# The residue value columns by seven block products, in turns with the plain ones

## The chip, the cores and the metric

The kernel runs on one core of a Trainium2 chip. The metric is device microseconds of one execution; the kernel before took 1865.35 us, the median of three runs (1864.94 to 1866.59).

## What is computed

A decoder trunk of two layers on x of 512 positions by 1024 channels, in float32. In each layer h = RMSNorm(x) is projected by one matrix w_in to queries and keys of a dilated attention (three head groups with dilations 1, 4 and 16), their values, and queries, keys and values of a retention, besides gates:

```
hn = rmsnorm(x, g_mix)
proj = hn @ w_in
qa, ka, va, qr, kr, vr, gr, ga, gb = jnp.split(proj, SPLIT_POINTS, axis=-1)
```

The attention's values va are three groups of 512 columns. Group 0 (dilation 1) is used in the order of the positions. Groups 1 and 2 (dilations 4 and 16) are used by residue: their tiles hold the positions t with the same t mod 4. The retention's values vr are 1024 columns in plain order. After that come the attention, the retention, w_a, w_b, w_o and a squared-ReLU MLP (w_up, w_down), which the change does not touch.

## The kernel before

**Products.** Every float32 operand is split in a high part, rounded to the matmul's fp32r format, and a low part, the rest. A product is three matmuls (high by high, high by low, low by high) that add up in PSUM. A weight unit is 128 partitions by 2048 columns (1 MB). ScalarE copies its two halves to w_hi (2 x 1.05 us) and VectorE subtracts to w_lo; there are two pairs of such buffers, so a unit is converted while the one before it is multiplied (`value_high`, line 844, waits for the end of unit n-2; `value_low`, line 1355). Raw weights land in the one buffer w_raw, each half of which may be loaded again when its low half is done.

**The value stage** is the first of each layer: a list of units, V_SEQ (line 76). G is group 0's value columns, two units of 48 matmuls of 128x512. P is vr, 1024 rows by 1024 columns: it is done by seven block products in Strassen's manner. Each of the seven takes a quarter of the activations, or a difference of quarters, by a quarter of the weights, or a sum of quarters, in 24 matmuls (4 k tiles x 2 position tiles x 3). R is groups 1 and 2 of va, in plain form: four halves (`residues_half`, line 2130) of 48 matmuls, whose stationary operand steps over h by 4 elements. The order is G G P1 R0 P5 R1 P6 P3 R2 P7 R3 P2 P4.

**The sums.** Quarters of h are subtracted on VectorE (`value_sum`, line 1361), then split by ScalarE (`set_high`, 859) and VectorE (`set_low`, 1376) into one of three sets. Products share PSUM banks: each result is read in between (`value_read` on ScalarE, 866, after products 1, 5, 6 and 4; `value_finish` on VectorE, 1382, after 3, 7 and 2), and `value_ready` (2095) makes TensorE wait for that read before it adds on or opens the bank anew. The sums of weight quarters are made by accumulating DMAs from GpSimd's queue (`add_values`, 1191) in two slots, gh[0] for products 1, 5, 6, 4 and gh[1] for 3 and 7; each waits until the slot's last content has been split. That is 4 accumulates of 1 MB a layer.

**SP's queue** issues in order: the units G, the two slots, x to scratch (two parts), raw R0 and R1, the store of rstd (after `rms_spread`) and its read back by residue, raw R2, R3, the scratch stores of vr (`vR_away`), raw P2, the tables, and then the first query and key pairs. VectorE's and ScalarE's loops over the stage (lines 1409 and 876) give, for each unit under way, the conversion of the next one and then reads, finishes and sums, all in order. TensorE takes the units one after the other (line 2155).

Of the kernel before, what the change touches and what calls it, by code (L numbers as in the profile page):

```python
# [35 lines left out]
P = 128  # L36
F32 = mybir.dt.float32
# [15 lines left out]
def trunk(nc, a):  # L53
# [54 lines left out]
    def by_raw(j):  # L108
        if j < P0:
            return V_SEQ[j - V0][0] != "P" or V_SEQ[j - V0][1] == 2  # L110
        return j < M0 or M_SEQ[j - M0][0] == "U" or plain(*M_SEQ[j - M0][1:])
# [22 lines left out]
    def last_read(l, i):  # L134
        return l * VO + TB + {3: 2, 7: 4, 2: 6}[i]

    def v_adds(l, i):
        return (l * 3 + {5: 1, 6: 2, 4: 3}[i] if i != 7 else l + 1) * 16

# [16 lines left out]
    with ExitStack() as ctx:  # L156
# [19 lines left out]
        nrstd = sb("nrstd", [P, TB], F32)  # L176
# [98 lines left out]
        diag = at("N", "diag", [P, TB, P], F32)  # L275
        hn = at("N", "hn", [P, 2, S], F32)
        relu = at("N", "relu", [P, 2, S], F32)
        gh = [at("N", f"gh{i}", [P, 2048], F32) for i in range(2)]
# [33 lines left out]
        def vbank(l, i):  # L312
            return ((sc, yr) if l > 0 else (yr, sc))[i in (5, 3, 2)]

        rbank = [pt[:, 0:S], pt[:, S:2 * S], pj[1][:], pj[0][:]]
# [85 lines left out]
        v_in = [sem(f"v_in{i}") for i in range(2)]  # L401
        v_added = [sem(f"v_added{i}") for i in range(2)]
        v_res = sem("v_res")
        v_first = sem("v_first")
# [93 lines left out]
        def _(sp):  # L498
# [35 lines left out]
            for l in range(0, DEPTH):  # L534
# [23 lines left out]
                def value_raw(kind, i):  # L558
                    d = raw[:].rearrange("p (k c) -> p k c", k=4)
                    v = value_block("R", i % 2, i // 2) if kind == "R" else value_block("P", 1, 0)  # L560
                    load(v_unit(l, kind, i), [(d[:, m:m + 2, :], v[:, m:m + 2, :]) for m in (0, 2)])

                def value_slot(slot):
                    sp.dma_start(gh[slot][:].rearrange("p (k c) -> p k c", k=4),
                                 value_block("P", slot, slot)).then_inc(v_in[slot], 16)
# [21 lines left out]
                def vR_away(part, m, b0):  # L587
                    if part < 3:
                        sp.wait_ge(v_out, last_read(l, (3, 7, 2)[part]))
                    else:  # L590
                        sp.wait_ge(v_first, first_read(l, 4))
# [28 lines left out]
                vR_away(1, 1, 2)  # L620
                sp.wait_ge(rot_out, l * 8 * PAIRS + 1)
# [127 lines left out]
        def _(act):  # L749
# [93 lines left out]
            for l in range(0, DEPTH):  # L843
                def value_high(s):
                    n = l * LU + V0 + s
                    act.wait_ge(mm_done, n * 2 - 2 + MM_CREDIT)
                    kind, i = V_SEQ[s] if s < VN else ("Q", 0)
                    if kind != "P" or i == 2:
                        hi_halves(n, n % 2)
                        return  # L850
                    slot = int(i in (3, 7))
                    if i in (1, 3):
                        act.wait_ge(v_in[slot], l * 16 + 16)
                    else:
                        act.wait_ge(v_added[slot], v_adds(l, i))
                    for c in HALVES:
                        nc.scalar.copy(w_hi[n % 2][:, c], gh[slot][:, c]).then_inc(hi_done, 1)  # L857

                def set_high(i):
                    p = V_SUMS.index(i)  # L860
                    if p >= SETS:
                        act.wait_ge(mm_done, v_unit(l, "P", V_SUMS[p - SETS]) * 2 + 2 + MM_CREDIT)
                    act.wait_ge(v_sum, l * 4 + p + 1)
                    nc.scalar.copy(a_sets[(p + 1) % SETS][0][:], ssum_v[p % 2]).then_inc(v_set_hi, 1)

                def value_read(i):
                    act.wait_ge(mm_done, v_unit(l, "P", i) * 2 + 2 + MM_CREDIT)
                    act.wait_ge(nrstd_done, l + 1)
# [3 lines left out]
                    for b in range(2):  # L872
                        nc.scalar.activation(vP[:, b0 + b, m], vbank(l, i)[:, b * S:(b + 1) * S], ACT.Copy,
                                             scale=by[:, b0 + b:b0 + b + 1]).then_inc(v_first, 1)

                for s in range(1, VN):
                    kind, i = V_SEQ[s]
                    if s == 2:
                        rms(l)
                    if V_SEQ[s - 1] in (("P", 1), ("P", 5), ("P", 6)):  # L880
                        value_read(V_SEQ[s - 1][1])
                    value_high(s + 1)
                    if (kind, i) in (("P", 1), ("R", 0), ("P", 5), ("P", 6)):
                        set_high({("P", 1): 5, ("R", 0): 6, ("P", 5): 3, ("P", 6): 7}[kind, i])
                value_read(4)
# [299 lines left out]
        def _(pool):  # L1185
# [4 lines left out]
            for l in range(0, DEPTH):  # L1190
                def add_values(i):
                    slot = int(i == 7)
# [3 lines left out]
                    nc.gpsimd.dma_start(gh[slot][:].rearrange("p (k c) -> p k c", k=4),  # L1196
                                        w_in_v[l, :, 4 * h:4 * h + 4, V_AT["P"] + m, :],
                                        accum_op=ALU.add).then_inc(v_added[slot], 16)

                for i in (5, 6, 4, 7):  # L1200
                    add_values(i)
# [41 lines left out]
        def _(dve):  # L1243
# [107 lines left out]
            for l in range(0, DEPTH):  # L1351
# [3 lines left out]
                def value_low(s):  # L1355
                    n = l * LU + V0 + s
                    kind, i = V_SEQ[s] if s < VN else ("Q", 0)
                    for hf in range(2):
                        lo_half(n, n % 2, hf, gh[int(i in (3, 7))] if kind == "P" and i != 2 else raw)

                def value_sum(i):
                    p = V_SUMS.index(i)
                    if p == 0:
                        dve.wait_ge(hn_done, 2 * l * KT + KT)
                        dve.wait_ge(sum_done, (2 * l + 1) * (KT - 1))
                    else:
                        dve.wait_ge(v_sum, l * 4 + p)
                    if p >= 2:
                        dve.wait_ge(v_set, l * 4 + p - 1)
                    a11, a12, a21, a22 = (h32[:, 4 * kh:4 * kh + 4, 2 * P * th:2 * P * th + 2 * P]  # L1370
                                          for th in range(2) for kh in range(2))
                    x0, x1, op = {5: (a21, a22, ALU.subtract), 6: (ssum_v[0], a11, ALU.subtract),
                                  3: (ssum_v[1], a12, ALU.add), 7: (a11, a21, ALU.subtract)}[i]
                    nc.vector.tensor_tensor(ssum_v[p % 2], x0, x1, op).then_inc(v_sum, 1)

                def set_low(i):
                    p = V_SUMS.index(i)
                    to_hi, to_lo = a_sets[(p + 1) % SETS]
                    dve.wait_ge(v_set_hi, l * 4 + p + 1)
                    nc.vector.tensor_tensor(to_lo[:], ssum_v[p % 2], to_hi[:], ALU.subtract).then_inc(v_set, 1)  # L1380

                def value_finish(i):
                    m, b0 = {2: (0, 0), 3: (1, 0), 7: (1, 2)}[i]
                    by, op = nrstd if i == 7 else rstd, ALU.add if i == 2 else ALU.subtract
                    dve.wait_ge(mm_done, v_unit(l, "P", i) * 2 + 2 + MM_CREDIT)
                    dve.wait_ge(v_first, first_read(l, {2: 1, 3: 6, 7: 5}[i]))
                    for b in range(2):
                        to = vP[:, b0 + b, m]
# [1089 lines left out]
```

## Time and profile before

| | |
|---|---|
| median of three runs | 1865.35 us |
| the profiled execution, in all | 1867.26 us |
| its span, first to last instruction | 1865.3 us |
| mean granted TensorE clock | 0.998 |
| TensorE, weight loads, VectorE, ScalarE, GpSimd busy | 1855.0, 1559.6, 1290.2, 832.5, 140.6 us |
| DMA moved | 236.9 MB, mean 127 GB/s |

A row of a timeline is the start in us, the duration, engine and line, operation, tile written from tiles read, and the count that was merged; the idle time before it and what ended it stand in brackets. DMA-issuing instructions stand on the queue that issues them (SPq, POOLq). A row of DMA issues has tile and source, queue, count, size of each, and the us from issue to landing. A windows row has the stretch, its length, the busy us and number of instructions of TensorE, its weight loads, VectorE, ScalarE and GpSimd, then the granted clock (1.00 is 2.4 GHz), the mean busy share of the 16 DMA engines and GB/s. A share slightly over 1 comes of packets that lie over the window's edge or each other.

### The profile page before, as it was taken

How to read it: one execution, taken by the hardware profiler on the slowest of the kernel's cores; microseconds unless marked ns; L12 is line 12 of the kernel's file. 1: busy time of each engine (PE TensorE's matmuls, PEld its weight loads, DVE VectorE, ACT ScalarE, POOL GpSimd, SP SyncE). 2: the span in 40 equal slices, each digit the busy share in tenths (PEclk: the TensorE clock that was granted, in tenths of full speed). 3: DMA queues.
4: the chain of work that ended last, by engine and by line, in shares of the span. 5: the costliest groups of instructions: out<-in, count | busy, mean ns of one | idle time of the engine just before them, and what ended most of it. 6: DMA issues, size and time to landing. Idle time of an engine off the chain costs nothing.

```text
span 1865.3 us, 22969 instructions
## 1 busy us (share of the span) xinstructions
PE 1855.0 (99%) x9016; PEld 1559.6 (84%) x9016; DVE 1290.2 (69%) x1882; ACT 832.5 (45%) x1234; POOL 140.6 (8%) x112
## 2 busy tenths in 40 slices
PE   9999999999999999999999999999999999999998
PEld 8988888888888888888889888888888888888886
DVE  6466878877446576776984668788675575667778
ACT  6335465465223343443543365554642234434345
POOL 0001111100000000000000112112000000000000
PEclk9999999999999999999999999999999999999999
DMA  8553233233433465557765433233243334655675
GB/s 255 125 167 110 75 86 105 84 94 96 133 96 125 117 148 133 145 135 189 174 181 149 137 92 97 77 111 96 69 147 100 104 113 113 136 142 140 142 205 137
DMA packets 213295, 236.92 MB, mean 127 GB/s; under 512 B 12354, under 2 KB 162626, under 8 KB 211908
## 3 DMA queue, kind: packets, MB, share of 16 engines
q1 hardware_dynamic: 191348, 192.64, 32.6%
q0 software_dynamic: 21120, 41.95, 13.3%
q8 instruction: 71, 1.16, 0.3%
q10 hardware_dynamic: 720, 0.87, 0.2%
q14 instruction: 36, 0.29, 0.1%
HBM read 222.72 MB, written 10.62 MB: 125 GB/s over the span
## 4 chain that ended last, share of the span: by engine, by line
PE 98%; DVE 1%; ACT 1%; DMA 0%; issue 0%; SPq 0%
PE pj L1986 21%; PE pj L1988 21%; PE pj L1987 21%; PE yr L2342 2%; PE yr L2346 2%; PE yr L2344 2%; PE sc L2342 2%; PE sc L2346 2%; PE sc L2344 2%; PE pt L2342 2%; PE pt L2344 2%; PE pt L2346 2%; PE sc L2190 1%; PE pt L2147 1%; PE pj L2147 1%; PE pt L2149 1%
## 5 line engine op out<-in xcount | busy, mean ns | idle before, releaser
L1986 PE MATMUL pj<-h_hi,w_hi 128*128 128x512 f32 x1408 | 554.0, 393 | 0.0
L1988 PE MATMUL pj<-h_hi,w_lo 128*128 128x512 f32 x1408 | 548.4, 389 | 0.0
L1987 PE MATMUL pj<-h_lo,w_hi 128*128 128x512 f32 x1408 | 548.2, 389 | 0.0
L759 ACT CAST w_hi<-w_raw 128x1024 fp32r<-128x1024 f32 x268 | 270.7, 1050 | 243.3 <-PE pj L1988 56.9
L1257 DVE TENSOR_TENSOR w_lo<-w_raw,w_hi 128x1024 fp32r<-128x1024 f32 x271 | 321.0, 1220 | 80.4 <-ACT w_hi L759 79.0
L1986 PEld LDWEIGHTS pj<-h_hi,w_hi 128*128 128x128 f32 x1408 | 264.3, 188 | 57.1 <-issue 1.9
L1988 PEld LDWEIGHTS pj<-h_hi,w_lo 128*128 128x128 f32 x1408 | 264.3, 188 | 56.0
L1987 PEld LDWEIGHTS pj<-h_lo,w_hi 128*128 128x128 f32 x1408 | 264.5, 188 | 53.9 <-issue 0.5
L1257 DVE TENSOR_TENSOR w_lo<-gh,w_hi 128x1024 fp32r<-128x1024 f32 x104 | 122.5, 1219 | 12.4 <-ACT w_hi L857 9.9
L1210 POOL TENSOR_TENSOR rcos<-rot,tables 128x512 f32<-128x512 f32 x64 | 88.5, 1384 | 524.1 <-ACT rot L893 465.6
L1067 ACT ACTIVATE relu<-pj 128x512 f32<-128x512 f32 x64 | 38.2, 597 | 182.6 <-PE pj L1988 182.6
L774 ACT CAST w_hi<-gh 128x1024 fp32r<-128x1024 f32 x80 | 80.0, 1050 | 87.5 <-PE yr L2346 35.5
L1752 DVE TENSOR_TENSOR u<-relu,rstd_all 128x512 f32<-128x512 f32 x64 | 44.1, 689 | 99.0 <-ACT relu L1067 98.9
L1218 POOL DMA_DIRECT2D gh<-in_w_down x26 | 33.4, 1283 | 937.3 <-DVE w_lo L1257 907.7
L893 ACT COPY rot<-pj 128x512 f32<-128x512 f32 x48 | 27.9, 582 | 102.1 <-PE pj L1988 56.3
L1451 DVE TENSOR_TENSOR swp<-swp,tables 128x512 f32<-128x512 f32 x64 | 65.0, 1015 | 4.4 <-ACT swp L897 2.7
L2342 PE MATMUL sc<-w_hi,a_hi 128*128 128x512 f32 x160 | 62.4, 390 | 0.3 <-DVE tables L1819 0.3
L2344 PE MATMUL sc<-w_lo,a_hi 128*128 128x512 f32 x160 | 62.3, 389 | 0.0
L2346 PE MATMUL sc<-w_hi,a_lo 128*128 128x512 f32 x160 | 62.2, 389 | 0.0
L2342 PE MATMUL yr<-w_hi,a_hi 128*128 128x512 f32 x160 | 62.2, 389 | 0.0
L2344 PE MATMUL yr<-w_lo,a_hi 128*128 128x512 f32 x160 | 62.2, 389 | 0.0
L2346 PE MATMUL yr<-w_hi,a_lo 128*128 128x512 f32 x160 | 62.2, 389 | 0.0
(352 smaller groups left out, 3199.5 us busy)
## 6 DMA issues: line engine op xcount, KB each, us to landing
w_raw<-in_w_in SPq DMA_DIRECT2D x139, 512.0 KB, 4.7
w_raw<-in_w_up SPq DMA_DIRECT2D x64, 512.0 KB, 4.6
gh<-in_w_down POOLq DMA_DIRECT2D x26, 1024.0 KB, 8.9
gh<-in_w_down SPq DMA_DIRECT2D x16, 1024.0 KB, 5.1
w_raw<-in_w_down SPq DMA_DIRECT2D x20, 512.0 KB, 5.2
gh<-in_w_in POOLq DMA_DIRECT2D x8, 1024.0 KB, 8.6
w_raw<-in_w_b SPq DMA_DIRECT2D x16, 512.0 KB, 4.4
w_raw<-in_w_o SPq DMA_DIRECT2D x16, 512.0 KB, 3.6
```

The lines of the kernel that those rows point to most:

```text
L759: nc.scalar.copy(w_hi[s][:, c], raw[:, c]).then_inc(hi_done, 1)
L774: nc.scalar.copy(w_hi[n % 2][:, h], gh[slot][:, h]).then_inc(hi_done, 1)
L1210: nc.gpsimd.tensor_tensor(rcos[:], rot[:], cosA if u < 3 else cosR, ALU.mult).then_inc(rot_cos, 1)
L1257: nc.vector.tensor_tensor(w_lo[s][:, c], src[:, c], w_hi[s][:, c], ALU.subtract).then_inc(lo_done, 1)
L1451: nc.vector.tensor_tensor(swp[:], swp[:], sinA if u < GROUPS else sinR, ALU.mult).then_inc(rot_sin, 1)
L1752: nc.vector.tensor_tensor(to, relu[:, o, :], rstd_all[:], ALU.mult).then_inc(relu_scaled, 1)
L1986: nc.tensor.matmul(out, w_hi[s][:, wc], acts[0], start=first, stop=False)
L1987: nc.tensor.matmul(out, w_hi[s][:, wc], acts[1], start=False, stop=False)
L1988: return nc.tensor.matmul(out, w_lo[s][:, wc], acts[0], start=False, stop=last)
L2342: nc.tensor.matmul(out, hi[:, k, t], w_hi[s][:, w], start=opens and k == 0, stop=False, skip_group_check=not opens)
L2344: nc.tensor.matmul(out, hi[:, k, t], w_lo[s][:, w], start=False, stop=False, skip_group_check=not opens)
L2346: return nc.tensor.matmul(out, lo[:, k, t], w_hi[s][:, w], start=False, stop=k == 3, skip_group_check=not opens)
```

## The change

R is gone. The residue columns of va are a second seven-product matrix, Q, that takes turns with P in the order 1 2 5 6 3 7 4: G G P1 Q1 P2 Q2 P5 Q5 P6 Q6 P3 Q3 P7 Q7 P4 Q4. Q1, Q2 and Q4 read h by residue as R did; the other four read sums which VectorE makes from h by residue, in four instructions each, and which lie contiguous. Q's banks are pj and pt. There are four weight slots: P's and Q's for 1, 5, 6, 4 and for 7; the new ones lie in the MLP's tiles and in the tables' tile, whose load now waits for Q7. Products 2 and 3 come raw. GpSimd issues eight accumulates. P2's finish and Q2's now stand before P5 and Q5, and rstd by residue is needed, negated too, from Q1's read on.

```
-    V_SEQ = [("G", 0), ("G", 1), ("P", 1), ("R", 0), ("P", 5), ("R", 1), ("P", 6), ("P", 3), ("R", 2), ("P", 7),
-             ("R", 3), ("P", 2), ("P", 4)]
+    V_SEQ = [("G", 0), ("G", 1)] + [(kind, i) for i in (1, 2, 5, 6, 3, 7, 4) for kind in "PQ"]
+    V_SUMS = [(kind, i) for i in (5, 6, 3, 7) for kind in "PQ"]
+    def v_slot(kind, i):
+        return 2 * (kind == "Q") + (i == 7)
+        v_slots = [gh[0][:], gh[1][:], v_q[:], tables[:].rearrange("p i s -> p (i s)")]
+        def vbank(l, kind, i, b):
+            if kind == "P":
+                return ((sc, yr) if l > 0 else (yr, sc))[i in (5, 3, 2)][:, b * S:(b + 1) * S]
+            return pj[b][:] if i in (5, 3, 2) else pt[:, b * S:(b + 1) * S]
...
 SP's queue:
-                value_slot(0)
-                value_slot(1)
+                value_slot("P", 1)
+                if l > 0:
+                    sp.wait_ge(a_ready, l * LD)
+                value_slot("Q", 1)
                 x_out(0)
-                value_raw("R", 0)
+                value_raw("P", 2)
                 x_out(1)
-                value_raw("R", 1)
+                value_slot("P", 7)
+                if l > 0:
+                    sp.wait_ge(d_turned, l * KT)
+                value_slot("Q", 7)
                 rstd_away()
                 rstd_by_residue()
-                value_raw("R", 2)
-                value_raw("R", 3)
+                value_raw("Q", 2)
+                value_raw("P", 3)
+                value_raw("Q", 3)
                 vR_away(0, 1, 0)
-                value_raw("P", 2)
                 vR_away(1, 1, 2)
+                sp.wait_ge(lo_done, v_unit(l, "Q", 7) * 2 + 2 + UNIT_CREDIT)
                 sp.wait_ge(rot_out, l * 8 * PAIRS + 1)
                 sp.dma_start(tables[:], a["tables"]).then_inc(tables_in, 16)
...
 ScalarE, during unit s:
+                    value_high(s + 1)
+                    if V_SEQ[s - 1][1] in (1, 5, 6) and V_SEQ[s - 1][0] == "P":
+                        value_read(*V_SEQ[s - 1])
+                    if s == V_SEQ.index(("Q", 2)):
+                        value_read("Q", 1)
+                    elif V_SEQ[s - 1] in (("Q", 5), ("Q", 6)):
+                        value_read(*V_SEQ[s - 1])
+                    if s + 2 < VN and V_SEQ[s + 2] in V_SUMS:
+                        set_high(*V_SEQ[s + 2])
...
 GpSimd:
-                    pool.wait_ge(lo_done, v_unit(l, "P", {5: 1, 6: 5, 4: 6, 7: 3}[i]) * 2 + 2 + UNIT_CREDIT)
+                    if i != 7:
+                        pool.wait_ge(lo_done, v_unit(l, kind, {5: 1, 6: 5, 4: 6}[i]) * 2 + 2 + UNIT_CREDIT)
                     pool.wait_ge(v_in[slot], l * 16 + 16)
-                for i in (5, 6, 4, 7):
-                    add_values(i)
+                for i in (5, 7, 6, 4):
+                    for kind in "PQ":
+                        add_values(kind, i)
...
 VectorE, during unit s:
+                    value_low(s + 1)
+                    if s == V_SEQ.index(("Q", 2)):
+                        dve.wait_ge(rstd_res, l * 16 + 16)
+                        negated(TB)
+                    if V_SEQ[s - 1][1] in (2, 3, 7) and V_SEQ[s - 1][0] != "G":
+                        value_finish(*V_SEQ[s - 1])
+                    if s + 2 < VN and V_SEQ[s + 2] in V_SUMS:
+                        set_low(*V_SEQ[s + 2])
+                    if s + 3 < VN and V_SEQ[s + 3] in V_SUMS:
+                        value_sum(*V_SEQ[s + 3])
...
 TensorE, value_ready:
+                    elif i in (5, 4):
+                        pe.wait_ge(v_last[kind], last_read(l, {5: 2, 4: 7}[i]))
                     else:
-                        pe.wait_ge(v_first, first_read(l, {6: 1, 7: 6, 3: 5}[i]))
+                        pe.wait_ge(v_first[kind], first_read(l, {6: 1, 7: 6, 3: 5}[i]))
```

## Rows read from the trace of the kernel before

**Rows 1.** Page: busy time, share of the span and instructions of each engine.
```profile
PE 1855.0 (99%) x9016; PEld 1559.6 (84%) x9016; DVE 1290.2 (69%) x1882; ACT 832.5 (45%) x1234; POOL 140.6 (8%) x112
```

**Rows 2.** Waits of TensorE, the longest: waited-for, us in total, times, longest.
```profile
PE pj L1950 <- DMA x_nat<-in_x: 1.2, 1, 1.2
```

**Rows 3.** Windows of the two value stages, layer 0 and layer 1.
```profile
35.30:119.70 84.40, 84.40 (x369) 77.68 (x370) 50.69 (x59) 29.84 (x34) 5.30 (x4) 1.00 0.58 142
957.30:1041.80 84.50, 84.50 (x371) 77.77 (x371) 49.39 (x57) 29.61 (x33) 3.85 (x3) 1.00 0.57 140
```

**Rows 4.** Timeline of TensorE: the first matmuls of R0, P5, R1, P6, P3.
```profile
41.65 0.62 PE L2147 MATMUL pt<-w_hi,h_hi 128*128 128x512 f32 x1
53.15 0.40 PE L2122 MATMUL sc<-w_hi,a_hi 128*128 128x512 f32 x1
58.63 0.40 PE L2147 MATMUL pt<-w_hi,h_hi 128*128 128x512 f32 x1
69.91 0.40 PE L2122 MATMUL yr<-w_hi,a_hi 128*128 128x512 f32 x1
75.36 0.39 PE L2122 MATMUL sc<-w_hi,a_hi 128*128 128x512 f32 x1
```

**Rows 5.** Timeline of VectorE and ScalarE: split, finish, plain and strided add; cast, read.
```profile
61.06 2.36 DVE L1257 TENSOR_TENSOR w_lo<-gh,w_hi 128x1024 fp32r<-128x1024 f32 x2 [2.01 <-ACT w_hi L857]
81.00 1.41 DVE L1389 SCALAR_TENSOR_TENSOR x<-sc,rstd,x 128x512 f32<-128x512 f32 x2 [0.85 <-PE sc L2126]
127.97 0.69 DVE L1456 TENSOR_TENSOR qk<-rcos,swp 128x512 f32<-128x512 f32 x1
138.77 1.06 DVE L1458 TENSOR_TENSOR qk<-rcos,swp 128x512 f32<-128x512 f32 x1
70.11 2.00 ACT L857 CAST w_hi<-gh 128x1024 fp32r<-128x1024 f32 x2 [8.12 <-PE pj L2149]
75.56 1.27 ACT L873 ACTIVATE x<-yr,rstd 128x512 f32<-128x512 f32 x2 [2.50 <-PE yr L2126]
```

**Rows 6.** Timeline of SP's queue: store of rstd and read back, both layers.
```profile
43.36 0.31 SPq L569 DMA_DIRECT2D rstd_scratch<-rstd_all  x1
46.92 0.37 SPq L573 DMA_DIRECT2D rstd<-rstd_scratch  x1
964.71 0.25 SPq L569 DMA_DIRECT2D rstd_scratch<-rstd_all  x1
967.60 0.36 SPq L573 DMA_DIRECT2D rstd<-rstd_scratch  x1
```

**Rows 7.** DMA issues at 35.95, 94.62, 41.62, 79.05, 80.18, 1814.39, 1817.22, in that order.
```profile
gh<-in_w_in POOLq DMA_DIRECT2D x1, 1024.0 KB, 8.6
w_raw<-in_w_in SPq DMA_DIRECT2D x1, 512.0 KB, 3.5
w_raw<-in_w_in SPq DMA_DIRECT2D x1, 512.0 KB, 4.3
w_raw<-in_w_in SPq DMA_DIRECT2D x1, 512.0 KB, 6.3
w_raw<-in_w_in SPq DMA_DIRECT2D x1, 512.0 KB, 6.5
u<-in_w_down POOLq DMA_DIRECT2D x1, 1024.0 KB, 12.5
w_raw<-in_w_down SPq DMA_DIRECT2D x1, 512.0 KB, 9.5
```

**Rows 8.** Windows: accumulate alone, beside plain loads, loads alone, beside again.
```profile
67.20:71.40 4.20, 4.20 (x20) 3.91 (x19) 1.29 (x2) 1.29 (x2) 0.00 (x0) 1.00 1.11 204
80.80:83.20 2.40, 2.40 (x12) 2.40 (x12) 1.41 (x2) 0.00 (x0) 0.00 (x0) 1.00 1.11 211
84.50:86.50 2.00, 2.00 (x10) 2.00 (x10) 1.00 (x1) 1.92 (x2) 0.00 (x0) 1.00 1.03 371
1819.00:1826.00 7.00, 7.00 (x32) 5.79 (x32) 6.70 (x7) 2.96 (x3) 0.00 (x0) 1.00 1.06 235
```

More of the change, by code:

```diff
@@ L400, in trunk @@
         st_lo = sem("st_lo")
[L401 to L404, printed above, removed]
+        v_in = [sem(f"v_in{i}") for i in range(4)]
+        v_added = [sem(f"v_added{i}") for i in range(4)]
+        v_first = {kind: sem(f"v_first_{kind}") for kind in "PQ"}
+        v_last = {kind: sem(f"v_last_{kind}") for kind in "PQ"}
         v_sum = sem("v_sum")
@@ L588, in vR_away @@
                     if part < 3:
-                        sp.wait_ge(v_out, last_read(l, (3, 7, 2)[part]))
+                        sp.wait_ge(v_last["P"], last_read(l, (3, 7, 2)[part]))
                     else:
-                        sp.wait_ge(v_first, first_read(l, 4))
+                        sp.wait_ge(v_first["P"], first_read(l, 4))
                     to = vr_scratch[:, 2 * m:2 * m + 2].rearrange("p h (b c) -> p b h c", b=TB)
@@ L1356, in value_low, with value_sum @@
                     n = l * LU + V0 + s
-                    kind, i = V_SEQ[s] if s < VN else ("Q", 0)
+                    kind, i = V_SEQ[s] if s < VN else ("G", 0)
                     for hf in range(2):
-                        lo_half(n, n % 2, hf, gh[int(i in (3, 7))] if kind == "P" and i != 2 else raw)
-                def value_sum(i):
-                    p = V_SUMS.index(i)
+                        lo_half(n, n % 2, hf, raw if kind == "G" or i in (2, 3) else v_slots[v_slot(kind, i)])
+                def value_sum(kind, i):
+                    p = V_SUMS.index((kind, i))
                     if p == 0:
@@ L1374, in value_sum @@
-                    nc.vector.tensor_tensor(ssum_v[p % 2], x0, x1, op).then_inc(v_sum, 1)
-                def set_low(i):
-                    p = V_SUMS.index(i)
+                    if p >= 2:
+                        dve.wait_ge(v_set, l * 8 + p - 1)
+                    if kind == "P":
+                        a11, a12, a21, a22 = (h32[:, 4 * kh:4 * kh + 4, 2 * P * th:2 * P * th + 2 * P]
+                                              for th in range(2) for kh in range(2))
+                        to = ssum_v[0]
+                    else:
+                        a11, a12, a21, a22 = (h32[:, 4 * kh:4 * kh + 4, :].rearrange("p k (m r) -> p k r m", r=4)
+                                              [:, :, 2 * th:2 * th + 2] for th in range(2) for kh in range(2))
+                        to = ssum_v[1].rearrange("p k (r m) -> p k r m", r=2)
@@ new lines, in value_sum @@
+                    x0, x1, op = {5: (a21, a22, ALU.subtract), 6: (to, a11, ALU.subtract),
+                                  3: (to, a12, ALU.add), 7: (a11, a21, ALU.subtract)}[i]
+                    if kind == "P":
+                        nc.vector.tensor_tensor(to, x0, x1, op).then_inc(v_sum, 1)
+                        return
+                    for k in range(4):
+                        mm = nc.vector.tensor_tensor(to[:, k], x0[:, k], x1[:, k], op)
+                    mm.then_inc(v_sum, 1)
@@ L1400, in first_values, with negated @@
                                                 ALU.mult).then_inc(v_out, 1)
[L1402 to L1407 removed]
+                def negated(c0):
+                    nc.vector.tensor_scalar(nrstd[:, c0:c0 + TB], rstd[:, c0:c0 + TB], -1.0, None,
+                                            ALU.mult).then_inc(nrstd_done, 1)
                 for s in range(1, VN):
[L1410 removed]
                     if s == 2:
@@ L2155, in _ @@
                 for kind, i in V_SEQ[V_U:]:
[L2156 removed]
+                    if (kind, i) == ("Q", 1):
                         spread(l)
[L2158 to L2162 removed]
+                    value_product(kind, i)
+                pe.wait_ge(v_last["Q"], (l + 1) * VO)
                 def queries_keys(i, behind=None):
@@ L2178, in scores @@
                         pe.wait_ge(rot_out, J * 8 + 6 + 1)
-                        pe.wait_ge(v_out, (l + 1) * VO)
-                        pe.wait_ge(v_first, (l + 1) * VF)
+                        for kind in "PQ":
+                            pe.wait_ge(v_first[kind], (l + 1) * VF)
+                            pe.wait_ge(v_last[kind], (l + 1) * VO)
                         pe.wait_ge(u_out, J * 4 + 4)
```

190 lines of the change are left out of this document (70 added, 120 removed).

## The prediction

> **What bounds the kernel now.** I read the page's totals first. TensorE is busy 1855.0 us, 99% of the span [rows 1], and its longest wait is 1.2 us, in the start-up [rows 2]. The path is TensorE's queue, so every matmul removed is worth its issue interval, until one of its feeders is late. The question is which feeder that will be. The value stage, which the change rebuilds, lasts 84.4 us in each layer. VectorE is busy 50.7 us of it, ScalarE 29.8 us, the DMA share is 0.58, and TensorE is gapless at the full granted clock, 1.00 [rows 3]. The timeline of TensorE gives the units: R0 starts at 41.65, P5 at 53.15, R1 at 58.63, P6 at 69.91, P3 at 75.36 [rows 4]; the stage ends at 119.7. A P product (24 matmuls) is 5.45 us (69.91 to 75.36), 0.227 us a matmul. A residue half (48 matmuls, 4-element steps in the stationary operand) is 11.28 us (58.63 to 69.91), 0.235 us a matmul; the first one took 11.50. The weight conversion for the next unit may start only when the unit before the present one has ended, as there are two pairs of buffers. In the long R halves that leaves 11.3 us for about 3.6 us of work; that slack is what the change spends.
>
> **Term A, the matmuls.** Removed in each layer: 4 R halves, 11.50 + 3 x 11.28 = 45.3 us. Added: 7 Q products. Three (1, 2, 4) read h by residue, at half a residue half: 5.85 + 2 x 5.64 = 17.1 us. Four read the contiguous sums: 4 x 5.45 = 21.8 us. Sum 38.9 us, so -6.4 us a layer. With nothing late the starts in layer 0 become: Q1 41.65, P2 47.50, Q2 52.95, P5 58.59, Q5 64.04, end 113.3.
>
> **What it costs beside TensorE.** Per layer three more units are converted, with 2.0 us on ScalarE and 2.3 on VectorE each [rows 5] (the row of two splits has 2.36, but the next instruction starts some 0.07 before such an end; the finish's 1.41 counts as 1.34 and a single split or sum as 1.14 likewise). There are four more sums, of four instructions each on residue-strided inputs. No row has one. The same 1024 elements contiguous take half of the 2.36 us of two splits, 1.2, while 512 elements with both inputs strided take 1.06 against 0.69 contiguous (the same rows). So a Q sum lies between 1.2 (no penalty) and 2.4 us (four times 0.53 and as many starts). I take 2.1, twice the strided row. Four more activation splits cost 1.05 us on ScalarE (half a cast's row) and 1.14 on VectorE each; two more finishes of 1.34, less eight R evictions. VectorE comes to 14 splits 32, 8 set lows 9, sums 4.6 + 8.4, six finishes 8, and the first values, norm and tables about 8: 70 us in a stage of 78. It fits as a total, but not as an order. Plain DMA: the weights for Q are two slots and two raw loads (4 MB, as R's four raw loads). New are four more accumulating DMAs of 1 MB, 8 in place of 4.
>
> **Term B, Q2's weights.** On SP's queue the raw load for Q2 now stands behind the store of rstd and its read back. Before, R1's load stood ahead of them (issued 41.62 and 42.76, ahead of 43.36). The store was issued at 43.36 and the read at 46.92 [rows 6], so SP stands 3.56 us. In the changed kernel rstd_all comes at about 42.6 (the spread is the same matmul, and VectorE is free of one sum), the read back at 46.2, and the two halves of Q2's load at 46.6 and 47.0. How long they take depends on what is under way. With no accumulate beside it such a half landed in 3.5 us, and at the tail of one in 4.3 [rows 7]. With one accumulate beside them for about 4 of the us they took 6.3 and 6.5. With one all the time (issued 1817.22) both took 9.5 [rows 7]. The reason is in the windows: an accumulate alone keeps the DMA share at 1.11 with 204 GB/s, and with plain loads beside it the sum is 211 to 235 GB/s, while plain loads alone move 371 [rows 8]. In the changed kernel accumulates for P5, Q5, P7, Q7 are queued from 35.95 on, the last three with no wait between them (at 42.1, when Q1 is split, then 43.4 and 44.7). 4.2 MB at 204 GB/s are 20.6 us; with the last part of slot Q7, Q2 and P3's load (2.3 MB) beside them at 235 GB/s, 27.7 us. So DMA is saturated from 38 to about 66, around Q2's load. I take the 9.5 row: the second half lands at T = 56.5.
>
> What hangs on T is VectorE's order, for P5 can't start before P2 is finished (its banks), and that finish now stands last in a chain: the cast of Q2's second half 1.05, ScalarE's high half of P5's sum 1.05 behind it, VectorE's low half 1.14, the sum for Q5 2.1, the split for P5 2.3, the negation 0.1, the finish 1.34, and about 0.4 for four handovers: 9.5 us. P5 starts at 56.5 + 9.5 = 66.0 in place of 58.6: **+7.4**. (Q2's own late start lies inside this.) At 3.5 to 4.3 us for the half it would be T = 51 and +2, or nothing if the sum is cheap; at T = 59, +10.
>
> **Term C, Q5.** It may not start before Q2 is finished. From P5's start: read of Q1 1.2 [rows 5] and set high 1.05 on ScalarE, then on VectorE set low 1.14, the sum for P6 1.14, the split for Q5 2.3, the finish 1.34, with handovers about 6.95 us, and P5 lasts 5.45: **+1.5**. It holds even where DMA is instant, as VectorE has no slack here; bounds 0.9 and 2.
>
> **Term D, P3 to P7.** P3 and Q3 are consecutive raw units. From P3's first split to Q3's: load 4.6, cast 1.05, split 1.22, handovers 0.2 = 7.0 us against 5.45, unless P3's was early, which VectorE (now behind) and Q6's accumulate forbid: +1.4. ScalarE, in order, then delays P7 by about the same, 1.3. The sum is **+2.7**; 0 if the accumulates run unhindered, 5 if they lag. P6 and Q6: the accumulate for P6 is issued at about 65, when P5 is split, and needs 8.6 [rows 7] plus 2.4 for cast and split: 76, against a start at 77.5. Hidden, by 1.5 us.
>
> Moved at no cost: the tables' load now waits for Q7's split and P7's finish, but is needed only for the first rotary some 6 us into the next stage; its splits are done before. The scratch stores of vP come later in units but no later against the end, and half of them are waited for only by the retention. The first R wait for four first values stays, as Q1's. PE's group waits on v_last are C and B.
>
> **Sum.** Layer 0: -6.4 + 7.4 + 1.5 + 2.7 = +5.2. Layer 1: the same stage and the same order. The store and read stood 2.9 us (964.71 to 967.60) in place of 3.56 [rows 6], so +4.6. Together +9.8 us. The profiled execution took 1867.3 us, 2 us outside its span and 1.9 above the median of 1865.35, so 1877 on its scale; on the median's, **1875 us**.
>
> Two rules of the Trainium skill bear on B. The trace shows 8.6 us for an accumulate of 1 MB. The page "DMA: Bandwidth & Descriptors", section "Anatomy of one DMA", gives 2.0 us plus the bytes over 436 GB/s for a DMA of this path, an estimate of 4.4 us here. By that nothing would queue and B and D would vanish; it is the first rival. The measurement disagrees for accumulates. The trace also shows plain loads slowed from 3.5 to 6.3 and 9.5 us beside one. The same page, "Issuing engines are not separate DMA queues", says that all issuers share the same 16 engines and interleave; the trace agrees.
>
> **Rivals.** (1) DMA keeps pace, faster: Q2's halves land in 4.3 us as R1's did at 41.62, so T = 51.3, P5 is late by 2.2, C 1.5, D 0: -2.7 a layer, **1860**; with no stall but C, -4.9, 1855.5. For it: the total DMA share is only 0.58, and R1's load met one accumulate's tail. Against it: three accumulates back to back, not one. It decides at T = 54.0 with D gone, at 51.3 with D whole. Chance 0.22. (2) Q2's load fares as the one at 79.05, 6.5 us: T = 53.5, B 4.4, D between 0 and 2.7: -0.5 to +2.2 a layer, **1867**. Chance 0.13. (3) The accumulates become the bound. Each behaves as the one at 1814.39, which took 12.5 us beside plain loads [rows 7]; four in a row from 38 then end at about 78, P6's lands at 84.5 and P6 starts at 86.9 in place of 77.5: +9.4 for D's 2.7: +11.9 a layer, **1889**. For it: 8 accumulates where 4 were. Against it: after 66 few plain loads are left. Chance 0.18. The forecast itself (1868.5 to 1884) has 0.47. That Q is not done by seven products at all is excluded by the diff.
>
> **Numbers.** A measurement of this kernel tells 0.2%, 3.7 us, from no change. Faster beyond it: rival 1, 0.22. Within: rival 2, 0.13. Slower: 0.65. The range 1857 to 1890 leaves out the best end of rival 1 and the upper half of 3.
>
> **What would show it.** A: 24 fewer 128x512 matmuls a layer in the value lines, at the same interval. B: a TensorE gap before the sixth unit (Q2) and before P5, with ScalarE waiting for w_raw from DMA, landings of 8 to 10 us at SP's load after the rstd read, and the P5 gap ended by VectorE's L1389 operation. C: a gap of 1 to 2 us before Q5, ended by the same line. D: gaps before Q3 and P7. A DMA share near 1 for 28 us. I am wrong if Q2's second half lands within 4.5 us of its issue, if the Q sums take 1.2 us, or if accumulates queued together move more than 204 GB/s.

## The result, and the profile after

The changed kernel took **1888.9 us** (median of 4 runs, 1888.0 to 1891.1) against 1865.8 for the kernel before on the same chip: ratio 1.0127, 95% interval 1.0115 to 1.0139, or +23.1 us. The forecast was 1875, +9.8. The direction was right, and the stalls stand where they were put, but the net loss is 2.4 times the forecast: the forecast had 11.6 us of stalls in layer 0 against 6.4 us of saved matmuls, and 18.0 came. The profiled execution took 1888.3 us. One execution of run 6 below took 3111 us at a mean granted clock of 0.556, a slower state of the chip, and its median leaves that one out.

The totals of the page of the changed kernel answer to [rows 1]:

```profile
PE 1851.6 (98%) x8968; PEld 1542.4 (82%) x8968; DVE 1329.4 (70%) x1932; ACT 861.6 (46%) x1270; POOL 151.3 (8%) x120
```

There are 48 matmuls fewer, 24 a layer, but TensorE's share of the span fell. Its waits, where there had been 1.2 us at most [rows 2] (waited for, us in total, times, longest):

```profile
PE pj L2151 <- DVE w_lo L1279: 16.0, 4, 6.2
PE sc L2151 <- DVE x L1422: 3.5, 1, 3.5
PE yr L2151 <- DVE x L1422: 2.8, 1, 2.8
```

The first is Q2's and Q3's weights, in both layers. The other two are P5, waiting for the finish of P2 (L1422; L1389 before). The windows of the two value stages (length, busy time and instructions of PE, PEld, DVE, ACT, POOL, granted clock, DMA share, GB/s) answer to [rows 3]:

```profile
33.04:129.08 96.04, 83.40 (x346) 69.98 (x346) 66.75 (x80) 42.99 (x50) 10.45 (x8) 0.93 0.76 175
966.71:1062.66 95.95, 83.33 (x346) 69.45 (x346) 66.71 (x80) 43.34 (x51) 9.05 (x7) 0.95 0.74 167
```

So 11.6 and 11.5 us more than 84.4 and 84.5: together the 23.1 of the medians. Nothing outside the value stages moved. (In the one profiled execution of before the stage starts 2.3 us later than here, and over 2 us later than in any other trace. That execution took 1.9 us more than its median, so the delay is taken to be its own.) TensorE's timeline in layer 0, the first matmuls of Q1, P2, Q2, P5, Q5, P6, Q3 and P7, answers to [rows 4]:

```profile
39.43 0.60 PE L2151 MATMUL pt<-w_hi,h_hi 128*128 128x512 f32 x1
45.27 0.40 PE L2151 MATMUL sc<-w_hi,h_hi 128*128 128x512 f32 x1
57.11 0.79 PE L2151 MATMUL pj<-w_hi,h_hi 128*128 128x512 f32 x1 [6.20 <-DVE w_lo L1279]
67.90 0.77 PE L2151 MATMUL sc<-w_hi,a_hi 128*128 128x512 f32 x1 [3.51 <-DVE x L1422]
76.26 0.39 PE L2151 MATMUL pj<-w_hi,a_hi 128*128 128x512 f32 x1
81.70 0.39 PE L2151 MATMUL yr<-w_hi,a_hi 128*128 128x512 f32 x1
99.64 0.47 PE L2151 MATMUL pj<-w_hi,a_hi 128*128 128x512 f32 x1 [1.46 <-DVE w_lo L1279]
106.20 0.47 PE L2151 MATMUL yr<-w_hi,a_hi 128*128 128x512 f32 x1 [0.84 <-DVE w_lo L1279]
```

The gap before Q2 is 6.2 us, the one before P5 is 3.5, and then P5 lasts 8.36 us without a gap, where such a product takes 5.45. SP's and POOL's queues, against [rows 6]. The start is the moment of issue. The last row merges six loads, the halves for Q2, P3 and Q3, issued between 44.86 and 92.5:

```profile
33.74 1.44 POOL L1217 DMA_DIRECT2D gh<-in_w_in  x1 [32.58 <-DVE w_lo L1279]
40.06 1.29 POOL L1217 DMA_DIRECT2D v_q<-in_w_in  x1 [4.89 <-DVE w_lo L1279]
40.82 1.84 POOL L1217 DMA_DIRECT2D gh<-in_w_in  x1
44.02 1.28 POOL L1217 DMA_DIRECT2D tables<-in_w_in  x1 [1.35 <-DMA tables<-in_w_in]
40.43 0.31 SPq L575 DMA_DIRECT2D rstd_scratch<-rstd_all  x1
44.45 0.37 SPq L579 DMA_DIRECT2D rstd<-rstd_scratch  x1
44.86 47.62 SPq L520 DMA_DIRECT2D w_raw<-in_w_in  x6
```

And how long they took to land (issued 33.74, 40.06, 40.82, 44.02; last Q2's two halves, a median), against [rows 7]:

```profile
gh<-in_w_in POOLq DMA_DIRECT2D x1, 1024.0 KB, 12.6
v_q<-in_w_in POOLq DMA_DIRECT2D x1, 1024.0 KB, 12.2
gh<-in_w_in POOLq DMA_DIRECT2D x1, 1024.0 KB, 18.6
tables<-in_w_in POOLq DMA_DIRECT2D x1, 1024.0 KB, 22.4
w_raw<-in_w_in SPq DMA_DIRECT2D x2, 512.0 KB, 11.4
```

The accumulates landed at 46.3, 52.3, 59.4 and 66.4, one each 6 to 7 us. The halves of Q2's load took 9.7 and 13.1 us, from 44.86 to 54.6 and from 45.44 to 58.5. ScalarE's casts show when the two halves of Q2's weights came, and VectorE's rows from there to the finish of P2 are the chain of the forecast, against [rows 5]:

```profile
54.67 1.04 ACT L771 CAST w_hi<-w_raw 128x1024 fp32r<-128x1024 f32 x1 [12.68 <-DMA w_raw<-in_w_in]
58.57 1.04 ACT L771 CAST w_hi<-w_raw 128x1024 fp32r<-128x1024 f32 x1 [2.85 <-DMA w_raw<-in_w_in]
61.92 2.21 DVE L1404 TENSOR_TENSOR fdiag<-h 128x256 f32<-128x256 f32 x4
64.06 2.35 DVE L1279 TENSOR_TENSOR w_lo<-gh,w_hi 128x1024 fp32r<-128x1024 f32 x2
66.40 1.40 DVE L1422 SCALAR_TENSOR_TENSOR x<-sc,rstd,x 128x512 f32<-128x512 f32 x2
```

The second half landed at 58.5, and P5 started 9.4 us later. The first window below is the stretch that the forecast called saturated: its DMA share is 1.06, so that part held. The others, from Q2's gap to Q5's end, show in the column before the DMA share a thing that the forecast doesn't have, against [rows 8]:

```profile
38.00:66.40 28.40, 20.19 (x84) 17.81 (x82) 13.88 (x17) 8.11 (x9) 3.88 (x3) 0.88 1.06 235
51.00:57.10 6.10, 0.00 (x0) 0.02 (x1) 1.22 (x1) 1.04 (x1) 0.00 (x0) 0.69 1.09 260
57.10:60.00 2.90, 2.89 (x7) 2.35 (x8) 0.36 (x1) 1.43 (x2) 0.00 (x0) 0.50 1.13 222
60.00:64.40 4.40, 4.39 (x19) 4.00 (x17) 4.40 (x7) 2.47 (x3) 0.00 (x0) 0.98 1.08 280
67.90:70.00 2.10, 2.10 (x5) 1.71 (x6) 1.20 (x2) 2.10 (x3) 0.08 (x1) 0.50 0.51 62
70.00:73.00 3.00, 3.00 (x8) 2.32 (x8) 3.00 (x4) 1.70 (x2) 0.00 (x0) 0.50 1.11 203
73.00:76.20 3.20, 3.20 (x13) 2.57 (x13) 3.20 (x5) 0.00 (x0) 1.28 (x1) 0.87 0.75 113
76.20:81.70 5.50, 5.50 (x26) 4.53 (x26) 5.20 (x7) 4.10 (x5) 1.11 (x1) 1.00 1.03 181
```

Behind each of the two gaps the granted clock is 0.50, the lower of TensorE's two levels: for about 3 us behind the first, more than 5 behind the second. TensorE is busy, with half the matmuls.

### The profile page after: what moved, and what is told of

The parts are those of the page before. It is cut to its first block, busy times and chain, and to the rows that moved or that the text cites. A ratio compares the mean times of both kernels' runs of the same rounds, so it can differ in the third digit from the quotient of the medians.

```text
span 1886.5 us, 23011 instructions
## 1 busy us (share of the span) xinstructions
PE 1851.6 (98%) x8968; PEld 1542.4 (82%) x8968; DVE 1329.4 (70%) x1932; ACT 861.6 (46%) x1270; POOL 151.3 (8%) x120
## 4 chain that ended last, share of the span: by engine, by line
PE 87%; DVE 5%; DMA 3%; ACT 2%; issue 2%; POOL 0%; SPq 0%; ACTq 0%; POOLq 0%
PE pj L2007 20%; PE pj L2008 20%; PE pj L2009 20%; PE yr L2349 2%; PE yr L2347 2%; PE yr L2351 2%; PE sc L2347 2%; PE sc L2349 2%; PE sc L2351 2%; DMA w_raw<-in_w_in 2%; PE pt L2349 2%; PE pt L2347 2%; PE pt L2351 2%; DVE w_lo L1279 1%; PE sc L2195 1%
## 5 line engine op out<-in xcount | busy, mean ns | idle before, releaser
L1279 DVE TENSOR_TENSOR w_lo<-w_raw,w_hi 128x1024 fp32r<-128x1024 f32 x267 | 317.0, 1221 | 100.8 <-ACT w_hi L771 99.3
L1279 DVE TENSOR_TENSOR w_lo<-gh,w_hi 128x1024 fp32r<-128x1024 f32 x100 | 117.8, 1220 | 1.4 <-ACT w_hi L786 1.3
L1472 DVE TENSOR_TENSOR swp<-swp,tables 128x512 f32<-128x512 f32 x64 | 66.4, 1037 | 4.4 <-ACT swp L917 2.7
```

The lines of the kernel that those rows point to most:

```text
L1279: nc.vector.tensor_tensor(w_lo[s][:, c], src[:, c], w_hi[s][:, c], ALU.subtract).then_inc(lo_done, 1)
L1472: nc.vector.tensor_tensor(swp[:], swp[:], sinA if u < GROUPS else sinR, ALU.mult).then_inc(rot_sin, 1)
```

## The experiments

Ratios are against the kernel before, with 95% intervals; diffs are against the changed kernel unless said. "Stage" is the value stage of layer 0 (84.4 before, 96.0 after).

**1. Q2's load ahead of the rstd trip**, the change's one new place on SP's queue undone.

```diff
+                value_raw("Q", 2)
                 rstd_away()
                 rstd_by_residue()
-                value_raw("Q", 2)
```

> SP's load of Q2's weights stands ahead of the rstd store and read, nothing else changed. Load theory (the queued accumulates keep DMA full, so Q2's weights land 9.8 and 13.2 us after their issue at 44.9, and every later gap follows): the issue moves some 2.5 us earlier but into the same saturated stretch, so about 2.5 us a layer, 1884. Queue-order rival (the load is late because SP waits for the rstd round trip): landing drops to 4 to 5 us, the gap before Q2 goes, 1868 to 1872. VectorE rival (its chain of splits, sums and finishes is too long whatever DMA does): no change, 1888.

1880.5 us, 1.0081 (1.0066 to 1.0096): 8.4 us back, more than the 1884 of the load theory and far less than the rival's. Issued 3.5 us earlier (41.40), the second half was cast 3.8 us earlier (54.77), and P5 started at 64.12, 9.3 us behind it. Position counts, one for one, but it is a third of the loss: the halves still take 9.3 and 12.2 us.

**2. The accumulates of P7 and Q7 later**, out of Q2's way.

```diff
-                for i in (5, 7, 6, 4):
+                for i in (5, 6, 7, 4):
```

> GpSimd issues the accumulates in the order 5 6 7 4 in place of 5 7 6 4, so that those for P7 and Q7 no longer stand around Q2's load. Load theory: Q2's halves land in about 6.5 us (one accumulate beside them) in place of 9.8 and 13.2, T comes 6 us earlier, and with the gaps the slow-clock stretches shrink: 6 to 7 us a layer, about 1875. Queue-order rival: unchanged, 1886 to 1889. VectorE rival: unchanged as well.

1889.5 us, 1.0128 (1.0113 to 1.0144): nothing gained, where 1875 was expected. Q2's halves took 7.1 and 7.9 us and were there by 53.2, and P5 started at 62.61, 9.4 us behind. But TensorE's longest wait is now Q3's:

```profile
54.48 0.62 PE L2151 MATMUL pj<-w_hi,h_hi 128*128 128x512 f32 x1 [3.74 <-DVE w_lo L1279]
97.31 0.77 PE L2151 MATMUL pj<-w_hi,a_hi 128*128 128x512 f32 x1 [5.69 <-DVE w_lo L1279]
```

The collision only moved, from Q2's raw load to Q3's, whose halves now took 9.3 and 12.1 us. Here P5 ran at the full clock to its end, and Q5 started 6.96 us after it: term C of the forecast, 6.95, by itself.

**3. Plain loads for the accumulates**: same queue, places and bytes, but the blocks are loaded over the slots, and the sums of weights are left out.

```diff
-                                        w_in_v[l, :, 4 * h:4 * h + 4, V_AT[kind] + m, :],
-                                        accum_op=ALU.add).then_inc(v_added[slot], 16)
+                                        w_in_v[l, :, 4 * h:4 * h + 4, V_AT[kind] + m, :]).then_inc(v_added[slot], 16)
```

> The eight accumulating DMAs of a layer's value stage become plain loads of the same blocks from the same queue (the weight sums are therefore left out). Load theory: a plain 1 MB load holds the DMA engines for about 2.8 us in place of 5 to 6, so Q2's load lands in 4 to 6 us, T = 50, P5 late by about 1.5 and Q5 by 1.5, the later raw unit by at most 1: between -2 and 0 us a layer against the kernel before, 1861 to 1866. If it is bytes and not accumulation that count: 1880 or more. VectorE rival: above 1880.

1872.6 us, 1.0041 (1.0027 to 1.0055), between the two outcomes expected. Without accumulation 16.3 of the 23.1 us are gone. Yet Q2's load, issued at 41.69, was cast at 53.61 and took 12 us, with a 5.6 us gap: plain bytes queued ahead of it do that too. What it repaired is the rest of the stage; apart from Q5's (term C) no wait behind P5 is over 0.4 us in layer 0 and 0.7 in layer 1.

**4. P2 and Q2 finished before the next split** on VectorE.

```diff
+                    if V_SEQ[s - 1][1] == 2:
+                        value_finish(*V_SEQ[s - 1])
                     value_low(s + 1)
...
```

> VectorE finishes products 2 (P2, Q2) before the next unit's split in place of after it; DMA is untouched. Load theory: the gap before Q2 stays (6.2 and 6.0 us), the one before P5 shrinks from 3.5 to about 1 us, as P5 now waits only for its split, and Q5's delay shrinks: 3 to 4 us a layer, about 1881. VectorE rival (its order is the main cause): the whole loss but the first gap goes, under 1876. Queue-order rival: no change.

1892.2 us, 1.0142 (1.0127 to 1.0157), no better than the change itself, where 1881 was expected. P5 came 8.2 us behind the load in place of 9.4, but Q5's split then stood behind the finish that it had stood ahead of, and Q5 waited 2.65 us in layer 0 and 1.0 in layer 1. An earlier finish by itself gains nothing.

**5. No accumulates for P7 and Q7** (those products use one block's weights).

```diff
-                for i in (5, 7, 6, 4):
+                for i in (5, 6, 4):
```

> The four accumulates for products P7 and Q7 of the two layers are left out (their weights are then unsummed; everything else as in the changed kernel). Load theory (a raw load of w_raw that meets queued accumulates is late): Q2's weights as in the run with those accumulates issued later, second half at about 53.2 in place of 58.6, P5 at that plus 9.4, and no gap at Q3 and P7 since nothing is moved there: 7 to 9 us a layer less than the changed kernel, 1871 to 1875. VectorE theory (its order alone makes the loss): 1885 or more.

1874.4 us, 1.005 (1.0035 to 1.0065), as expected. Without four of the sixteen accumulates 14.5 us are gone, though Q2's weights still came at 54.2 in layer 0. (The gains of the runs overlap and don't add up: runs 3 and 5 remove some of the same accumulates.)

**6. Sums ahead of the awaited conversions** of Q2 and Q3, on both engines.

```diff
+                    late = s + 1 < VN and V_SEQ[s + 1] in (("Q", 2), ("Q", 3))
+                    if late:
+                        set_low(*V_SEQ[s + 2])
+                        value_sum(*V_SEQ[s + 3])
                     value_low(s + 1)
```

> While the raw weights of Q2 (and of Q3) are awaited, ScalarE and VectorE do the next split and sum of activations first, in place of after that conversion; DMA untouched. The chain from Q2's second half to P5 loses set high, set low and the Q sum, 9.4 down to about 6.4 us, while Q2 itself starts and ends as before, so the gap before P5 (3.5 us) falls to under 1 and its slow-clock matmuls to half: 3 to 4 us a layer, 1881 to 1883. If VectorE's order were the main cause, under 1876; if only the load counts, 1888.

1883.9 us, 1.0103 (1.0087 to 1.012): 4 to 5 us back, with intervals that just overlap. P5 lost its wait, while Q2's grew to 6.9 us and Q3's to 3.3.

**7. The slots of P7 and Q7 loaded and added before P2's raw load**, with POOL's order 7, 5, 6, 4.

```diff
+                value_slot("P", 7)
+                value_slot("Q", 7)
                 value_raw("P", 2)
                 x_out(1)
-                value_slot("P", 7)
-                value_slot("Q", 7)
```

> The two slot loads for products 7 are issued before P2's raw load, and GpSimd issues their accumulates first, so that they run in the last G unit and the backlog of four ends some 6 us earlier. Load theory: Q2's second half lands 5 to 6 us earlier (at about 53 in place of 58.6), no collision is moved to Q3: 6 to 8 us a layer, 1873 to 1877, unless G1's or P2's weights are late now. VectorE theory: no change.

1887.3 us, 1.0119 (1.0104 to 1.0134), nothing, where 1873 to 1877 was expected: Q2 waited 6.6 us and P5 started at 68.07. The four accumulates did end 6 us earlier, at 60.5 in place of 66.4, but Q2's halves took 10.0 and 13.7 us all the same. Accumulates were still under way beside them until they had landed (58.7), as in the changed kernel; what stood in the queue behind that moment made no difference.

**8. Runs 1, 6 and 7 together.**

> The three changes together: Q2's load ahead of the rstd trip, slots and accumulates of products 7 early, activation sums ahead of the awaited conversions. If load and chain add up: Q2's second half at about 51, P5 at 57.5 to 58 (nominal 56.3), Q5 1.5 later, 1 at the end, so 4 us of the 6.4 saved are lost: about -2 us a layer, 1861 to 1866, as fast as the kernel before or a little faster. If DMA stays full for the whole stage whatever the order: 1872 or more.

1878.4 us, 1.0073 (1.0056 to 1.009), over the 1861 to 1866 hoped for. P5 came 6.1 us behind the load, but Q2 waited 3.2 us and Q3 3.2. While the raw tile was handed from P2 to Q2 and from P3 to Q3, no reordering that was run gave back more than 10.5 of 23 us.

**9 and 10. No load of their own for Q2, and for Q2 and Q3**: they convert what P2 (and P3) left in the raw tile, so those weights are the wrong blocks. Run 10, of which 9 is the half:

```diff
-                value_raw("Q", 2)
+                sp.wait_ge(lo_done, v_unit(l, "Q", 2) * 2 + 2 + UNIT_CREDIT)
...
-                value_raw("Q", 3)
+                sp.wait_ge(lo_done, v_unit(l, "Q", 3) * 2 + 2 + UNIT_CREDIT)
...
+                    if kind == "Q" and i in (2, 3):
+                        for c in HALVES:
+                            nc.scalar.copy(w_hi[n % 2][:, c], raw[:, c]).then_inc(hi_done, 1)
+                        return
```

> Q2 has no load of its own: it is converted from w_raw as P2 left it (its weights are then P2's), P3's load follows later; all accumulates, slots and orders as in the changed kernel. Load theory: the gap before Q2 goes (6.2), P5 is late by at most 1.5, its matmuls run at the full clock, Q5 1.5; what is left is the gap before Q3 with P7 (2 to 3.5). Per layer 9 to 11 us less than the changed kernel, 1867 to 1871. VectorE theory: P5 and Q5 keep 5 us of their lateness, 1875 or more.

> Neither Q2 nor Q3 has a load of its own (they are converted from what P2 and P3 left in w_raw). Load theory: the stage is then bound by matmuls and by the waits for the finish of Q2 alone: 78.05 us plus 1.5 to 3, so 80 to 81 against 84.4 before, 1857 to 1860, faster than the kernel before by what the removed matmuls are worth less 1.5 to 3 us a layer. VectorE theory: not under 1866.

Run 9: 1868.6 us, 1.0017 (1.0008 to 1.0026). Run 10: **1861.0**, 0.9975 (0.9965 to 0.9984), under the kernel before. Run 9 is as expected, run 10 one us over it. So 20.3 us hang on Q2's load and 7.5 on Q3's. (These runs also move 1 or 2 MB less a layer; runs 13 and 14 move all of it.) What was left in both were waits for P6's accumulate, behind those of P7 and Q7 (2.8 to 2.9 us in layer 0, 0.7 to 0.8 in layer 1), and one of 0.9 us before Q5; run 9 still had Q3's (2.5 and 2.2).

**11 and 12. Tiles of their own**: the whole computation, with Q2's weights in a part of vA that is filled late, loaded from 28.7 us on, and Q3's in half of h32; POOL's order 5, 6, 7, 4. Run 12 has the sums of P6 and Q6 behind Q2's finish too.

```diff
+        v_own = {2: vA[:, :, 2 * AW:3 * AW], 3: h32[:, 4:8, :]}
...
+                sp.dma_start(v_own[2], value_block("Q", 1, 0)).then_inc(v_in[4], 16)
                 rstd_away()
...
-                value_raw("Q", 3)
+                sp.wait_ge(v_sum, l * 8 + 6)
+                sp.dma_start(v_own[3], value_block("Q", 1, 1)).then_inc(v_in[5], 16)
```

> The whole computation, with tiles of their own for the raw weights of Q2 (the part of vA that Q5 and Q6 write later) and Q3 (the half of h32 that no later sum reads). Q2's load is issued right after x is stored, before the rstd trip; the slots of products 7 come after that trip, their accumulates after those of 6; Q3's load when the sum for Q3 is done. Load theory: Q2's weights land 2 to 5 us before they are needed, and Q3's too: as the run without these loads, 80 to 82 us a stage, 1857 to 1862. If DMA is full for the whole stage, other transfers (P3's, Q6's sum) are late in their place: 1866 or more.

> As e11_own_tiles, and VectorE makes the sums for P6 and Q6 behind the finish of Q2 in place of the first of them ahead of it. The wait of Q5 for that finish (1.5 us in the prediction) loses 1.1 us: 1 us a layer less than e11_own_tiles, 1855 to 1860; if P6's sum is late in its place, the same or 1 us more.

1879.2 us, 1.0069 (1.0056 to 1.0082), and 1877.8, 1.0062 (1.0049 to 1.0074): both missed what was expected (1857 to 1862 and 1855 to 1860). Q2 and P5 had no wait at all. Nearly the whole loss was one wait a layer, with Q3 slowed behind it (6.9 us for 5.45), the first row below (TensorE's timeline of run 11); the second, of SP's queue, is its cause:

```profile
93.93 0.76 PE L2166 MATMUL pj<-w_hi,a_hi 128*128 128x512 f32 x1 [9.50 <-DVE w_lo L1393]
77.34 0.37 SPq L632 DMA_DIRECT2D h<-in_w_in  x1
```

Half of h32 is free only after the sixth sum, at 77.3, and the load issued then took 14.1 us, with three accumulates under way.

**13 and 14. Every load early.** From run 11: Q2's weights and then P3's in the part of vA, Q3's in the raw tile, which P2 leaves at about 43; ScalarE reads Q5 behind P3's split, as Q5's values go where P3's weights stood. Run 14 has run 12's order of sums as well.

```diff
-                value_raw("P", 3)
-                sp.wait_ge(v_sum, l * 8 + 6)
-                sp.dma_start(v_own[3], value_block("Q", 1, 1)).then_inc(v_in[5], 16)
+                sp.wait_ge(lo_done, v_unit(l, "Q", 2) * 2 + 2 + UNIT_CREDIT)
+                sp.dma_start(v_own, value_block("P", 1, 1)).then_inc(v_in[5], 16)
+                value_raw("Q", 3)
```

> The whole computation; as the version with own tiles, but Q2's weights and then P3's take turns in the part of vA that Q5 and Q6 fill late, and Q3's take the raw tile, which P2 leaves at 42 us; Q5's read on ScalarE moves behind P3's split. In the version with own tiles TensorE's one long wait per layer was 9.5 us for Q3's weights, whose load could be issued only at 77.3 us, when the sixth sum had left its tile. Theory (what costs the time is that a load is issued only one or two products before its weights are wanted, behind what is queued on the 16 engines): both waits go and nothing takes their place, 1879.2 - 2 x 9.5 = 1860 us (1858 to 1864), faster than the kernel before. Rival (the transfers as a whole can't keep up with seven products a pair, wherever they are put): the wait comes back at another product of the same stage, 1870 us or more.

> The same with the sums of P6 and Q6 on VectorE behind Q2's finish, which took away a wait of 0.9 us before Q5 in the version with own tiles. Theory: 1858 to 1862 us, 0 to 1.5 us under its neighbour. Rival: 1870 us or more, as above.

1855.2 us, 0.9943 (0.993 to 0.9955), and **1853.1**, 0.9934 (0.992 to 0.9948): 0.6 and 0.7% under the kernel before, and under what was expected. Run 14, window of the stage in layer 0 and the longest wait before its end:

```profile
32.94:111.91 78.97, 78.42 (x346) 67.27 (x346) 66.47 (x80) 43.32 (x51) 10.48 (x8) 1.00 0.90 213
PE yr L2174 <- DVE w_lo L1291: 0.3, 1, 0.3
```

The same matmuls, bytes and eight accumulates a layer as in the changed kernel run with no stall over 0.3 us, at a DMA share of 0.90 and the full clock, in 79.0 us (78.2 in layer 1). P3's load still took 8.7 us and Q3's halves 10.1; they were issued at 48.8 and 49.3 for casts at 73.4 and 78.8.

## Why the prediction was wrong

**Term A, -6.4 us a layer: right.** Q1 to P2 took 5.84 us (5.85 forecast) and Q5 to P6 5.44 (5.45). Run 14, where little else is left, is 12.5 us under the kernel before, and twice 6.4 is 12.8.

**Term B: right in mechanism, mis-sized by 4.2 us in layer 0 and 4.6 in layer 1. This is the step that failed.** It said +7.4 at P5; measured from P1's start, P5 was 11.6 us late. The chain from the landing to P5 was 9.4 us (9.5), the Q sum in it 2.21 (2.1). What failed is the sentence "I take the 9.5 row". The first half took 9.7 us, as priced, but the one that counts is the second, and it took 13.1: 3.6 of the 4.2 us. In the 9.5 row both halves met one accumulate, which landed with them (1826.9, against 1826.8 and 1827.8), and nothing was queued behind it. Q2's load, issued at 44.86, met the tail of one (landed 46.3) and three more (52.3, 59.4, 66.4), so that no part of it ran alone. The forecast had counted that queue (27.7 us of saturation), and then took the time of a transfer that had met one of them. Run 1 shows that issuing earlier hardly shortens the transfer, run 7 that a backlog that ends 6 us earlier doesn't either as long as it outlasts the load, and runs 2 and 3 that with fewer accumulates or none 7 to 12 us remain. The second half was also issued 0.7 us later than forecast, counted from P1, mostly as SP stood 4.0 us for the rstd trip in place of 3.6. The forecast's own working gives the measured delay for a landing so late: counted from P1 it came at its T = 60.8, and for T = 59 it has +10.

**Term C, +1.5: right by itself, +2.9 in layer 0 of the change.** Runs 2 and 3, with P5 at the full clock, have Q5 6.96 us after P5 (6.95 forecast). (The steps that the forecast lists add up to 8.2 us; they fit from the read of Q1 on, which stands 1.3 us ahead of P5.) In the changed kernel the finish that Q5 waits for was done by 74.7, and P5 itself lasted until 76.2 at the granted clock of 0.50 behind the 3.5 us gap. The forecast priced gaps by their length alone.

**Term D, +2.7: 3.6 in layer 0, 4.8 in layer 1, and its first part agrees by luck.** P3 to Q3 took 7.06 us where the forecast has 7.0 from P3's first split to Q3's (less 5.45 that is 1.6, not its 1.4). But from split to split it was 8.5 us (89.72 to 98.26), as the load took 6.1 us beside an accumulate in place of 4.6, and the first half of P3's weights had been split 1.6 us before P3 started, which the forecast had excluded. The two errors cancel. P7 followed 6.57 us later (6.75), and 0.8 came at the stage's end, where the next unit's weights were late and no stall was foreseen. In layer 1 P3 itself was 0.9 us late and Q3 came 8.05 us after it.

So layer 0 is -6.4 + 11.6 + 2.9 + 3.6, and layer 1 -6.4 + 11.4 + 1.7 + 4.8: 11.6 and 11.5 us by the unrounded rows, together 23.1. The excess over the forecast's 5.2 in layer 0 is 4.2 (B), 1.4 (clock) and 0.9 (D); over its 4.6 in layer 1 it is 4.6 (B), 0.2 (clock) and 2.1 (D).

**P6 hidden by 1.5 us: held, only because all before it was late.** Without the early stalls (runs 9 and 10) P6 waited 2.8 and 2.9 us for its accumulate in layer 0; with POOL's order 5, 6, 7, 4 and early loads 0.3 (run 14). (The start it was held against, 77.5, is 78.4 by the forecast's own terms.)

**The rivals.** The third's total, 1889, is the one measured, but by luck: it put 9.4 us of delay at P6, and P6 had no wait. (Its four accumulates at 12.5 us from 38 on would end at 88, not at 78 as it says; measured, they ended at 66.4.) The first, that DMA keeps pace, is wrong for this order of issue and right for the engines: run 14 moves all of it without a stall over 0.3 us. As for the Trainium skill's "DMA: Bandwidth & Descriptors", section "Anatomy of one DMA", by which 1 MB takes an estimated 4.4 us: the accumulates took 12.2 to 22.4 us here from issue to landing when queued, and 8.5 to 8.7 one at a time. The measurement decides. What the Trainium skill's same page says under "Issuing engines are not separate DMA queues", that all issuers share the 16 engines, the traces bear out: in run 3 plain loads of POOL's queue held up SP's load as well (12 us for a half, where one took 3.5 before with nothing beside it).

**Open.** How much of the loss the halved clock makes was not isolated, as no two runs differ in the clock alone. 1.4 us in layer 0 is read off P5's length. In layer 1 P5 was 7.15 us long (the clock 0.76 over it), 0.2 more than term C's 6.95, so there it cost less. Nor is it shown how the DMA engines divide their time between the two queues; the landings alone are.

## What to carry to other kernels

A load that may be issued only when its predecessor's tile is free has a lead of one or two units. When units get shorter (here 11.3 to 5.5 us), count that lead against the landing time in all the traffic that will be under way until it lands, not against a landing in the traffic of before. If it doesn't cover, find the load a tile that is free earlier. Reordering the queues or the engines' work moved the stall between Q2, P5, Q5 and Q3 in six runs (1, 2, 4, 6, 7 and 8); a free tile, found in an output region that is filled late, took it away.

## What the runs showed of the hardware

- TensorE's granted clock went from 1.00 to 0.50 (2.4 to 1.2 GHz) in or behind gaps of 1.9 to 9.5 us, and was back only after about 3 to 6 us of full work. It need not fall in the gap: the first row is P5 in run 1, from 1.9 us behind a gap of 3.77 (0.89 over those 1.9). The second is Q3 in run 11, right behind the 9.5 us; the third P6 in run 10, behind a gap of 2.89 that left the clock alone. The fourth is Q3 in run 5, behind a gap of only 2.03, so the length of the gap before it does not tell by itself; Q3 in run 1 (1.90) and in layer 1 of run 9 (2.24) were slowed too, and Q3 in layer 1 of the changed kernel (2.37) was not. The gap of 2.8 us before P5 in that layer had 0.76 over P5 behind it; Q2's gap of 6.0 stood 11 us ahead of that one.

```profile
66.00:69.00 3.00, 3.00 (x9) 2.35 (x8) 3.00 (x4) 1.95 (x2) 0.00 (x0) 0.50 1.12 205
93.90:96.00 2.10, 2.07 (x5) 1.71 (x6) 1.42 (x2) 2.10 (x4) 0.00 (x0) 0.50 0.00 0
71.40:74.00 2.60, 2.60 (x12) 2.12 (x13) 1.91 (x2) 1.63 (x4) 1.28 (x1) 1.00 0.45 80
96.00:98.50 2.50, 2.50 (x7) 1.94 (x7) 1.93 (x3) 2.43 (x3) 0.00 (x0) 0.50 0.00 0
```

- A 2 KB transfer suffers too: the read back of rstd took 1.7 us before, 5.8 in the changed kernel and 8.3 behind plain loads in run 3.
- Four additions or subtractions of 128 by 256 residue-strided f32 elements took 2.21 us on VectorE, where one of 128 by 1024 contiguous ones takes 1.22.
